# Dense products of a three-layer transformer in plain FP32 by pairs of 64 stationary columns, with ten weight slots that TensorE reads itself and eight expert slots

## The reference

```
for l in range(2):
    u = x @ w_in[l]                     # 1024 -> 28 x 256 columns
    y_a = silu(layer_norm(conv31(a * sigmoid(g)))) @ w_conv_out[l]
    y_b = diff_attention(...) @ w_diff_out[l]
    y_c = block_attention(...) @ w_moba_out[l]
    m = sigmoid gates * (y_a, y_b, y_c), summed
    x = layer_norm(ALPHA * x + m @ w_o[l])
    h = square(relu(x @ w_ff1[l] + b_ff1[l]))          # 4096 wide
    x = layer_norm(ALPHA * x + h @ w_ff2[l] + b_ff2[l])
h = rms_norm(x); proj = h @ w_in_2
y_a = sparse_attention(top-64 keys) @ w_proj_a_2
y_b = gated_mlp(...) @ w_proj_b_2
x = x + (sigmoid(ga) * y_a + sigmoid(gb) * y_b) @ w_out_2
h2 = rms_norm(x)
for e in range(32):                     # top 2 of 32 experts for a token
    he = silu(h2 @ w_gate[e]) * (h2 @ w_up[e])
    y = y + comb[:, e] * (he @ w_down[e])
return rms_norm(x + y)
```

## Time and profile before

| what | value |
|---|---|
| time, median of 3 runs | 1489.43 us (1488.13 to 1491.2) |
| the profiled execution | 1489.11 us, span 1487.4 us |
| PE busy | 1351.1 us, 91% |
| PEld busy | 1180.9 us, 79% |
| DVE busy | 875.0 us, 59% |
| ACT busy | 599.7 us, 40% |
| read from memory | 289.71 MB, 197 GB/s over the span |

### The profile page before, as it was taken

One profiled execution on the slowest core, in us unless ns is written; L12 is line 12 of the kernel. 1 busy time (PEld: TensorE's weight loads), 2 busy tenths in 40 slices (PEclk: granted clock), 3 DMA queues, 4 the chain that ended last, 5 costly groups with the idle time before them and its releaser, 6 DMA issues.

```text
span 1487.4 us, 24986 instructions
## 1 busy us (share of the span) xinstructions
PE 1351.1 (91%) x9634; PEld 1180.9 (79%) x9634; DVE 875.0 (59%) x1414; ACT 599.7 (40%) x929; POOL 34.9 (2%) x52
## 2 busy tenths in 40 slices
PE   3699998989999899999989999879799779999996
PEld 3699998979889799998969998678789656666663
DVE  2399975765555689986775555656864532221213
ACT  2235665444444344566344444434453412111111
POOL 1000000000000000000000000020140000000000
PEclk9899999999999899999999999989999869999998
DMA  7674433645556355443546555464345459999992
GB/s 219 126 237 143 157 117 102 219 154 189 195 169 197 116 188 195 142 149 100 163 132 223 183 186 195 135 203 127 117 136 194 174 208 368 391 393 380 392 394 103
DMA packets 174927, 294.16 MB, mean 198 GB/s; under 512 B 10340, under 2 KB 143092, under 8 KB 162548
## 3 DMA queue, kind: packets, MB, share of 16 engines
q1 hardware_dynamic: 170128, 285.15, 56.0%
q0 software_dynamic: 1776, 4.97, 1.4%
q10 hardware_dynamic: 2932, 2.82, 1.4%
HBM read 289.71 MB, written 3.21 MB: 197 GB/s over the span
## 4 chain that ended last, share of the span: by engine, by line
PE 65%; DVE 18%; issue 7%; ACT 5%; DMA 3%; ACTq 1%; DVEq 0%; SPq 0%
PE ps L1534 15%; PE ps L1535 14%; PE ps L1536 14%; PE ps L1915 8%; DVE w_lo L986 6%; PE ps L1901 4%; PE ps L1929 4%; ACT w_hi L624 3%; DMA raw<-in_w_in 2%; DVE cv L1102 2%; PE ps L1938 2%; ACTq L618 1%; DVE x_nat L1048 1%; DMA cv<-in_rel_bias 1%; DVE ps L1059 1%
## 5 line engine op out<-in xcount | busy, mean ns | idle before, releaser
L986 DVE TENSOR_TENSOR w_lo<-raw,w_hi 128x2048 fp32r<-128x2048 f32 (+1 forms) x170 | 378.5, 2226 | 199.6 <-ACT w_hi L624 199.0
L624 ACT ACTIVATE w_hi<-raw 128x2048 fp32r<-128x2048 f32 (+1 forms) x170 | 316.8, 1863 | 275.8 <-PE ps L1536 247.1
L1534 PE MATMUL ps<-xT_hi,w_lo 128*128 128x256 f32 (+1 forms) x1224 | 357.3, 292 | 4.1 <-DVE xT_lo L1239 2.2
L1535 PE MATMUL ps<-xT_lo,w_hi 128*128 128x256 f32 (+1 forms) x1224 | 349.6, 286 | 0.0
L1536 PE MATMUL ps<-xT_hi,w_hi 128*128 128x256 f32 (+1 forms) x1224 | 349.4, 285 | 0.0
L1534 PEld LDWEIGHTS ps<-xT_hi,w_lo 128*128 128x128 f32 (+1 forms) x1224 | 237.4, 194 | 15.1 <-issue 11.6
L1535 PEld LDWEIGHTS ps<-xT_lo,w_hi 128*128 128x128 f32 (+1 forms) x1224 | 237.4, 194 | 0.5
L1536 PEld LDWEIGHTS ps<-xT_hi,w_hi 128*128 128x128 f32 (+1 forms) x1224 | 237.0, 194 | 0.2
L1534 PE MATMUL ps<-w_hi,xT_lo 128*128 128x256 f32 (+2 forms) x560 | 172.3, 308 | 16.2 <-DVE w_lo L986 15.8
L1535 PE MATMUL ps<-w_lo,xT_hi 128*128 128x256 f32 (+2 forms) x560 | 169.5, 303 | 0.0
L1536 PE MATMUL ps<-w_hi,xT_hi 128*128 128x256 f32 (+2 forms) x560 | 169.3, 302 | 0.0
(11 more groups left out here) (334 smaller groups left out, 1943.3 us busy)
## 6 DMA issues: line engine op xcount, KB each, us to landing
raw<-in_w_in SPq DMA_DIRECT2D x72, 1024.0 KB, 5.2
raw<-in_w_ff SPq DMA_DIRECT2D x64, 1024.0 KB, 5.4
qkT<-in_w_gate SPq DMA_DIRECT2D x16, 1024.0 KB, 12.5
raw<-in_w_down SPq DMA_DIRECT2D x16, 1024.0 KB, 10.7
raw<-in_w_gate SPq DMA_DIRECT2D x16, 1024.0 KB, 13.0
w_exp<-in_w_up SPq DMA_DIRECT2D x16, 1024.0 KB, 15.2
w_exp<-in_w_down SPq DMA_DIRECT2D x16, 1024.0 KB, 11.4
raw<-in_w_o SPq DMA_DIRECT2D x8, 1024.0 KB, 5.0
```

The lines of the kernel that those rows point to most:

```text
L624: nc.scalar.activation(w_hi[:, u % SPLIT, 0:n], raw[:, u % RAW, 0:n], ACT.Copy).then_inc(hi_done, 1)
L986: nc.vector.tensor_tensor(w_lo[:, u % SPLIT, 0:n], raw[:, u % RAW, 0:n], w_hi[:, u % SPLIT, 0:n].bitcast(F32), ALU.subtract).then_inc(spli ...
L1534: nc.tensor.matmul(out_, left[1], right[0], start=start, stop=False)
L1535: nc.tensor.matmul(out_, left[0], right[1], start=False, stop=False)
```

## The change

All splitting is gone, with its buffers and semaphores. One float32 array `xT`, one `br`, and a ring `raw` of ten slots, from which PE reads the weights directly: it waits for the slot's arrival, and SP loads a slot again once PE has finished with it (`unit_done`). Every dense product, and the values, column sums and latent scores with 128 stationary columns, goes through `halves`: two plain float32 matmuls, stationary columns 0 to 63 and 64 to 127, each into its half of the output rows. Transposed activations are copied from PSUM by ACT and DVE in turn, and factors of 0.5 move into copies. The normed rows of the experts are written once, by DVE, in the permuted order. Gather and scatter are one product each instead of a high and a low one. The experts have eight slots. The router's product puts tokens on the output rows, which takes a copy and two transposes away. The loops over layers, feed-forward turns and experts are written out.

```diff
-RAW, SPLIT = 4, 2
-RAW_CREDIT, SPLIT_CREDIT = RAW, SPLIT
+SLOTS = 10
+CREDIT = SLOTS
...
-DUOS, RING = 3 * PAIRS, 6
+DUOS, RING = 3 * PAIRS, 8
...
-            def mm3(out_, left, right, start, stop):
-
-                nc.tensor.matmul(out_, left[1], right[0], start=start, stop=False)
-                nc.tensor.matmul(out_, left[0], right[1], start=False, stop=False)
-                return nc.tensor.matmul(out_, left[0], right[0], start=False, stop=stop)
+        def halves(out_, left, right, start, stop):
+
+            for e in range(2):
+                part = slice(e * HD, (e + 1) * HD)
+                last = nc.tensor.matmul(out_[part], left[:, part], right, start=start, stop=stop)
+            return last
...
-            def load(base, u, dst, src):
-
-                sp.wait_ge(split_done, base + u + 1)
-                sp.dma_start(dst, src).then_inc(raw_in[u % RAW], 16)
+            def load(g, k, n, src, at=0):
+
+                if at == 0:
+                    sp.wait_ge(unit_done, g + 1)
+                dst = unit3(raw, g % SLOTS, k, n)
...
+                sp.dma_start(dst, src).then_inc(raw_in[g % SLOTS], 16)
...
-                nc.scalar.activation(w_hi[:, u % SPLIT, 0:n], raw[:, u % RAW, 0:n], ACT.Copy).then_inc(hi_done, 1)
...
-            def weights(u, k, n):
-                return unit3(w_hi, u % SPLIT, k, n), unit3(w_lo, u % SPLIT, k, n)
+            def weights(g, k, n):
+
+                pe.wait_ge(raw_in[g % SLOTS], arrived(g))
+                return unit3(raw, g % SLOTS, k, n)
...
                     for m in range(4):
                         k = 4 * g + m
-                        for n, x in enumerate((h2_hi, h2_lo)):
-                            for a in range(TT):
-                                last = nc.tensor.matmul(ps[:, XG_B, m * P:(m + 1) * P], x[:, a, k * P:(k + 1) * P], picks[:, a, q], start=n == 0 and a == 0, stop=n == 1 and a == TT - 1)
+                        for a in range(TT):
+                            last = halves(ps[:, XG_B, m * P:(m + 1) * P], h2[a][:, k * P:(k + 1) * P], picks[:, a, q], a == 0, a == TT - 1)
...
                         for a in range(TT):
-                            for k, y in enumerate((y_lo[h], y_hi[h])):
-                                last = nc.tensor.matmul(ps[:, ACC + 2 * a + h, :], place[d % 2][:, a, :], y, start=d == 0 and k == 0, stop=d == PAIRS - 1 and k == 1)
+                            last = halves(ps[:, ACC + 2 * a + h, :], place[d % 2][:, a, :], y_sb[h], d == 0, d == PAIRS - 1)
```

More of the change, by code:

```diff
@@ L90, with load_inc, arrived @@
 X_IX, X_TOP, X_QL, X_LNV, X_SP, X_YB, X_S = 4, 6, 8, 8, 10, 11, 11
[L93 to L103, removed]
+def load_inc(g):
+    if g >= G2:
+        return 16 * LOADS.get(g - G2, 1)
+    return 48 if U_BR <= g % UNITS < U_WO else 16
+def arrived(g):
+    return sum(load_inc(v) for v in range(g % SLOTS, g + 1, SLOTS))
 CONSTS, BCASTS = 11 * 16, 6 * 16
-ACT_LINKS, DVE_LINKS = 1, 93
 def bc(ap, axis, n):
@@ L945, in moe_round @@
-                for g in range(2):
-                    gather_copy(0, g)
-                moe_steps(act, step)
+                        gather_copy(p + 1, 1)
+                    act.wait_ge(y_done, plus(p + 1, PAIRS))
+                    if p >= 1 or r is not None:
+                        act.wait_ge(scattered[0], plus(p, PAIRS))
+                    nc.scalar.activation(y_sb[0], ps[:, Y_BANKS[0], :], ACT.Copy).then_inc(y_c[0], 1)
             moe_round(None)
@@ L1547, in transposed, with natural @@
                     for k in range(KC):
[L1548 to L1551 removed]
+                        if done is not None and c == 0 and k % 2 == 0:
+                            ready_xT(done, k // 2)
+                        last = halves(ps[:, bank, c * T:(c + 1) * T], w[:, k, c * P:(c + 1) * P], xT[:, k, :], k == 0, k == KC - 1)
                 last.then_inc(unit_done, 1)
[L1554 to L1556 removed]
+            def natural(g, bank, n=256, between=None):
+                w = weights(g, KC, n)
                 for a in range(TT):
@@ L1569, in rows_unit @@
                         for k in range(2):
-                            last = mm3(ps[:, ACC + 2 * a + h, :], [x[:, k, a * P:(a + 1) * P] for x in left],
-                                       [x[:, k, h * BANK:(h + 1) * BANK] for x in w], start and k == 0, stop and k == 1)
+                            last = halves(ps[:, ACC + 2 * a + h, :], left[:, k, a * P:(a + 1) * P], w[:, k, h * BANK:(h + 1) * BANK], start and k == 0, stop and k == 1)
                         if stop and (a, h) != (TT - 1, 1):
@@ L1749, in bank_free @@
                     pe.wait_ge(ev2, w - 2)
-            make_xT2(0)
+            make_xT2(0, [hn[:, a, :] for a in range(TT)])
             def small(w, half):
@@ L1961, in moe_round @@
                 pe.wait_ge(rowsT_c, 1)
-                moe_steps(pe, step)
+                for p in range(PAIRS):
+                    inner(p, 0)
+                    inner(p, 1)
+                    if p < PAIRS - 1:
+                        gather(p + 1, 0)
+                    if p >= 1:
+                        scatter(p - 1)
+                    pe.wait_ge(he_ready, plus(p + 1, PAIRS))
+                    for c in range(2):
+                        last = nc.tensor.transpose(ps[:, GU_B, c * P:(c + 1) * P], he[:, p % 2, c * P:(c + 1) * P], ident[:])
+                    last.then_inc(heT_done, 1)
+                    if p < PAIRS - 1:
+                        gather(p + 1, 1)
+                    outer(p)
                 scatter(PAIRS - 1)
```

830 lines of the change are left out of this document (293 added, 537 removed).

## The result

The changed kernel takes 1650.32 us (median of 4 runs, 1646.74 to 1651.88) against 1489.30 before (1488.13 to 1491.20). The ratio is 1.1076, with a 95% interval of 1.1055 to 1.1098: 10.8% slower. The forecast was 1678 us within 1645 to 1715. Sign and mechanism held, and the size was 28 us too high.

The account below looks back on a forecast made before the run. The prediction took PE to bound the kernel throughout: 1489 us plus 140, 65 and 25 for dearer products and scatter, less 17, 10, 8, 3.5 and 2 for recovered waits, gave 1678 us, range 1645 to 1715.

Parts of the forecast that it names:

- The product: Dense products: a pair of plain float32 halves takes 0.432 us at 256 columns, 0.864 at 512.
- Rivals 1 and 4: Dense products: 1, pairs are cheap, about 1110 us, 4%; 4, halves run one after the other, near 2800 us, 1%.
- 256 and 512 columns, +205 us: Dense products: 1920 of 256 columns, from 0.359 to 0.432 us, +140; 352 of 512, from 0.679 to 0.864, +65.
- Scatter, +25: Experts: eight passes of 1.91 us a step become four products of 3.46 us; 16 x 1.55 = +25 us.
- gather's: Experts: 8 products become 16 instructions of 64 columns, 1.6 to 2.6 us a group against 1.93; no change taken.
- the start's term: Start: the 14.7 us stand for a low half and 2.5 us of half clock behind it come back, 17 us.
- Idle time, 38 us of the sum: PE's waits at start, second block, layers, transposed activations and router: 17, 10, 8, 3.5 and 2 us taken back.
- in the second block: Before the experts: 10 us of PE's 17.7 us idle time come back, bounds 0 and 17.7.
- in the layers: Projections and feed-forward parts of both layers: half of 17 us idle comes back, 8 us.
- at the router: Router: low half of normed rows, a copy and two small transposes go; 2 us back, nothing as lower bound.
- the 3.5 us forecast for the copies of the transposed activations: ACT copy and DVE subtraction become one copy split between the engines: 0.7 us less at each of 5 places.
- Signs named beforehand: Profile after: PE about 94% busy, DVE under 35%, ACT under 20%, no stand near 60 us, experts' queue below 370 GB/s.

Follow-up runs that it names:

- the fourth experiment: Kernel before, with the 2 MB store of the bias table in four pieces, later and on GpSimd's queue: 1470.19 us, ratio 0.9883.
- the fifth experiment: Changed kernel, with a weight unit loaded at most four units ahead of TensorE instead of ten: 1661.45 us.
- the second experiment: Kernel before, its three float32r passes replaced by one plain FP32 matmul on the high parts, splits still made: 1660.76 us.
- the third experiment: Changed kernel, with each dense product of weights as three float32r passes on a small constant array, values left out, waits kept: 1455.80 us.
- the sixth experiment: Changed kernel, but in units of 256 moving columns all products of the first 64 stationary columns precede the second's: 2088.39 us.

## Why the prediction was right, and where it was 28 us off

**The product.** The price, 0.432 us for a pair at 256 columns, is what the changed kernel shows within 0.3% (220.55 us for 221.2 where the clock was full). Nor is it four of the float32r passes of before, 0.480: a quarter of it is 0.108 us, where such a pass took 0.120. The Trainium skill's FP8 and Floating Point Precision, section TensorE Precision Notes, with its four passes for true FP32, agrees with the traces if a pass is taken as 0.108, and not if it is taken from the kernel before. Rivals 1 and 4 fall with it. The feed-forward pair of units is 13.8 us, as written.

**256 and 512 columns, +205 us.** Measured with the splits kept: +196. The step that failed is the price of before: 0.359 us came from steps inside a unit. Taken from start to start over the whole program, with the units' ends and the half-clock stretches in it, the 1920 products of 256 columns took 718.9 us as three passes, 0.374 each, and 849.9 as whole plain products, 0.443. That is +131 where the sum had +140. The 352 products of 512 columns took 242.3 us (0.688 each) and 303.0 (0.861): +61 where the sum had +65. I had added nothing to the steps inside a unit, and what had to be added was larger before. The rest of the 196 is spread over small products.

**Scatter, +25.** 16 steps, 17.79 - 16.28 each: +24. From start to start the scatter's records alone took 56.6 us for 31.0, and gather's 58.5 for 63.5, where no change was forecast. The 3.7 us by which PE is busier with pairs than with whole products had not been in the sum.

**The clock, 2.5 us in the start's term.** This is the term that was mis-sized most. Work lost to half clock fell by 34.9 - 16.3 = 18.6 us. At the start it fell by 0.9 us only (2.6 to 1.7). Some 11 us of it went with the stands of 1 to 5 us in the second block (four stretches of 1.7 us) and behind the branch products (1.6 and 2.7). I had counted those stands as idle time and left the slower work behind each of them out. Another 4.5 us (11.4 to 6.9) went behind the last norm and the router's wait, where the stands are still there; why it was less there stays open. So 196 + 24 + 3.7 - 18.6 = 205 us more of busy time; the trace has 206.6 (the first and third of these hold some 1 us of clock each, in opposite directions).

**Idle time, 38 us of the sum (17 + 10 + 8 + 3.5 + 2, less the 2.5).** 45.9 came back. By the stands of over 0.7 us: at the start 11.8 (14.67 to 2.89), where I had 14.7; in the second block 16 (six stands of 1.32 to 4.60 us, one of 0.86 left), where I had taken 10 between 0 and 17.7; in the layers 8 (three stands of 1.27 to 2.04 us in each, one of 0.73 left), as forecast; at the router about 1, forecast 2; at the norms about 1. Stands under 0.7 us make up the rest, and the 3.5 us forecast for the copies of the transposed activations can't be told apart in it.

**What this makes together:** 9 us less dense work, 16 more of clock and 8 more of idle time are 33 us; the pairs' 4 and roundings leave the 28. The mechanism was right: PE is the bound, and its dearer products outweigh all that comes back. The sizes of the dense price, the clock and the idle time were off, all in one direction.

**The reasons for the gains.** That the start's stand was the store's, and worth 17 us, is shown by the fourth experiment (18.1 us). The changed kernel avoids only part of it, by loading early; the fifth experiment shows that this is all that ten slots do. The two expert slots were called worthless, and are. That DVE's splits cost only PE's waits held too, but in part these waits would have shrunk anyway: the second experiment gets 23.9 us of idle time back with every split in place.

**Signs named beforehand:** PE 95% busy (94 forecast), DVE 27%, ACT 15%, one short stand of 2.9 us at 63.7 us instead of none, the experts' queue at 372 GB/s where under 370 was written.

## What to carry to other kernels

Take the price of an operation from start to start over whole stages, not from the middle of a burst, when hundreds of units hang on it. Beside TensorE's idle time itself, price the slower clock that follows each stand: here 35 us before and 16 after; where a stand can't be removed, products that nobody reads can bridge it. And ask of a change that removes work from engines beside the bound what it makes dearer on the bound itself: 424 us less on VectorE and 356 less on ScalarE were worth at most 57 us of time by the third experiment (32.5 and the scatter's 24, and the ten slots have their share in it), and the product they were traded for cost 196.

## What was not expected of the hardware

- A whole plain product with 128 stationary columns and a pair of 64 cost the same within 0.1% (220.39 and 220.55 us for a feed-forward part at full clock).
- Halves of the array that do not stand side by side in the program still overlap for four records at each change of half: in the sixth experiment (one run) that makes 52 steps of 0.216 us for the 64 records of a unit, 11.2 us, where no overlap would be 13.8.
- 184 small products of 0.216 us, put into TensorE's waits, made the program 12.9 us shorter, with a mean granted clock of 0.998 instead of 0.980.
